# Delta rules: no dense products in the first seven steps of the meta tokens' chain, more of them in the four tiles' steps

## The reference, cut to what matters

```python
def gated_delta_rule(q, k, v, g, beta):          # chunks of 64, 8 heads
    ...
    kb = k * beta[..., None]
    lower = jnp.where(strict, jnp.einsum('nbhid,nbhjd->nbhij', kb, k) * decay, 0.0)
    rhs = jnp.concatenate([v * beta[..., None], kb * jnp.exp(g)[..., None]], axis=-1)
    sol = lax.linalg.triangular_solve(eye + lower, rhs, left_side=True, lower=True)
    u, w = sol[..., :DV], sol[..., DV:]
    ...
    def step(S, xs):
        v_new = u_c - jnp.einsum('bhcd,bhde->bhce', w_c, S)
        o = jnp.einsum('bhcd,bhde->bhce', qd_c, S) + jnp.einsum('bhij,bhje->bhie', attn_c, v_new)
        S = S * gl_c[..., None, None] + jnp.einsum('bhcd,bhce->bhde', kd_c, v_new)
        return S, o
```

## Time and profile before

| | us |
|---|---|
| median of 3 runs | 2184.63 |
| lowest and highest | 2182.49, 2186.39 |
| the profiled execution | 2186.5 |
| its span | 2184.7 |
| its mean granted TensorE clock | 0.984 |
| TensorE busy in the span | 2103.3 (96%) |
| first group's `delta_rule` | from 876.5 to 1061.6 |
| second group's `delta_rule` | from 1289.1 to about 1471 |

### The profile page before, as it was taken

One profiled execution on the slowest core, in us unless ns is written; L12 is line 12 of the kernel. 1 busy time (PEld: TensorE's weight loads), 2 busy tenths in 40 slices (PEclk: granted clock), 3 DMA queues, 4 the chain that ended last, 5 costly groups with the idle time before them and its releaser, 6 DMA issues. The chain is left out here.

```text
span 2184.7 us, 32900 instructions
## 1 busy us (share of the span) xinstructions
PE 2103.3 (96%) x13936; PEld 1681.0 (77%) x13936; DVE 1098.9 (50%) x1676; ACT 821.8 (38%) x1326; POOL 66.0 (3%) x69
## 2 busy tenths in 40 slices
PE   8979999999999899999999999999999899999999
PEld 6757678888888798666789976669786678888887
DVE  4544765777743366445355645444437544444422
ACT  4324554444432274222433532226436433222211
POOL 0011320000000000000000000000000000000000
PEclk9999999999999999999999999999999999999999
DMA  4331002333333321111223211113220232333222
GB/s 171 107 106 49 1 30 77 97 97 97 97 97 97 106 81 56 59 40 40 97 87 127 78 49 50 40 30 118 88 68 1 97 126 87 96 97 96 93 92 96
DMA packets 51426, 175.69 MB, mean 80 GB/s; under 512 B 6480, under 2 KB 10960, under 8 KB 50640
## 3 DMA queue, kind: packets, MB, share of 16 engines
q1 hardware_dynamic: 51280, 173.59, 24.6%
HBM read 164.07 MB, written 8.45 MB: 79 GB/s over the span
## 5 line engine op out<-in xcount | busy, mean ns | idle before, releaser
L280 PE MATMUL ps<-nx_hi,whi 128*128 128x512 f32 (+3 forms) x1696 | 574.8, 339 | 13.0 <-PEq L2204 6.3
L281 PE MATMUL ps<-nx_lo,whi 128*128 128x512 f32 (+3 forms) x1696 | 571.7, 337 | 0.0
L282 PE MATMUL ps<-nx_hi,wlo 128*128 128x512 f32 (+3 forms) x1696 | 570.7, 336 | 0.0
L266 ACT ACTIVATE whi<-raw 128x1024 fp32r<-128x1024 f32 x282 | 297.4, 1054 | 591.6 <-PE ps L282 545.8
L275 DVE TENSOR_TENSOR wlo<-raw,whi 128x1024 fp32r<-128x1024 f32 x282 | 344.4, 1221 | 261.0 <-ACT whi L266 260.7
L280 PEld LDWEIGHTS ps<-nx_hi,whi 128*128 128x128 f32 x1696 | 322.1, 190 | 57.2 <-DVE wlo L275 7.2
L281 PEld LDWEIGHTS ps<-nx_lo,whi 128*128 128x128 f32 x1696 | 321.9, 190 | 33.8
L282 PEld LDWEIGHTS ps<-nx_hi,wlo 128*128 128x128 f32 x1696 | 322.2, 190 | 33.4
L280 PE MATMUL ps<-mixer_out,whi 128*128 128x512 f32 x384 | 154.0, 401 | 5.8 <-PEq L2888 3.8
L282 PE MATMUL ps<-mixer_out,wlo 128*128 128x512 f32 x384 | 153.1, 399 | 0.0
L281 PE MATMUL ps<-mixer_out,whi 128*128 128x512 f32 x384 | 153.1, 399 | 0.0
(11 more groups left out here) (456 smaller groups left out, 2778.3 us busy)
## 6 DMA issues: line engine op xcount, KB each, us to landing
raw<-stream_dram SPq DMA_DIRECT2D x285, 512.0 KB, 3.5
arena<-keys_dram SPq DMA_DIRECT2D x1, 2112.0 KB, 9.3
h_sb<-x_dram SPq DMA_DIRECT2D x4, 512.0 KB, 6.7
mixer_floats<-cmp_w_k_dram SPq DMA_DIRECT2D x8, 256.0 KB, 4.0
mixer_floats<-cmp_w_v_dram SPq DMA_DIRECT2D x8, 256.0 KB, 4.5
h_dram<-h_sb SPq DMA_DIRECT2D x1, 2048.0 KB, 8.6
gate_dram<-arena SPq DMA_DIRECT2D x1, 2048.0 KB, 7.2
keys_dram<-h_sb SPq DMA_DIRECT2D x1, 2048.0 KB, 9.2
```

The lines of the kernel that those rows point to most:

```text
L266: act.activation(K.whi[:, n % HL], K.raw[:, n % RAW], ACT.Copy).then_inc(K.s_hi, 1)
L280: pe.matmul(out, whi, xhi, start=start, stop=False, skip_group_check=skip)
L281: pe.matmul(out, whi, xlo, start=False, stop=False, skip_group_check=skip)
L282: return pe.matmul(out, wlo, xhi, start=False, stop=stop, skip_group_check=skip)
```

## The change

The weights of the first seven points of the meta chain become zero; the eighth, "u_sb", keeps its 6. `SIDE_X` stays as it is. As the 360 dense matmuls of a group are shared out over a smaller sum of weights, the four tiles' points and "u_sb" get what the seven points no longer take.

```diff
-SIDE_META = {"ug": 4, "lower": 8, "a_sb": 4, "x2_sb": 4, "a4_sb": 4, "x8_sb": 4, "r_sb": 4, "u_sb": 6}
+
+SIDE_META = {"ug": 0, "lower": 0, "a_sb": 0, "x2_sb": 0, "a4_sb": 0, "x8_sb": 0, "r_sb": 0, "u_sb": 6}
 SIDE_X = {"ug": 4, "lower": 12, "a_sb": 4, "x2_sb": 4, "a4_sb": 4, "x8_sb": 4, "r_sb": 4, "k_sb": 4, "k2_sb": 4, "y_sb": 4,
           "w_sb": 4, "nw": 3, "vn 0": 4, "state 1": 4, "vn 1": 4}
```

## The result

The changed kernel takes 2199.34 us (median of 6 runs, 2196.12 to 2201.43) against 2184.53 of the kernel before (6 runs): the ratio is 1.0065, interval 1.0054 to 1.0077. It is slower, as forecast, but beyond the top of the range (2198.0). Two later comparisons gave 1.0051 (1.0037 to 1.0064) and 1.0058 (1.0046 to 1.0071). All runs of this study together have medians of 2198.5 (16 runs) and 2186.1 (93 runs), 12.4 us apart.

What follows compares the result with a forecast made beforehand. TensorE, busy 96%, was taken to bound the kernel through idle stretches and clock. Per group 1.6 us (8.0 tiles minus 6.4 meta chain) plus 3.3 for the clock, twice, made 9.7 on 2184.6: 2194, range 2187.5 to 2198.

Steps and rivals of the forecast that it cites:

- The tiles' term: In the four tiles: 37 moved dense matmuls cost 8.6 us, with changed idle stretches 8.0 us per group.
- tile 1's 1.87: Ahead of tile 1's L2314: a 1.87 us idle stretch, expected to go since no chunk ends at tile 0's end.
- rival (c): In each group one eviction in its new place isn't covered, 1.9 us on top: 2198; chance 0.05.
- The meta chain's latency: Meta chain without dense matmuls runs at its own latency: L2300 at 882.8 against 889.17, saving 6.4 us per group.
- the small batches: Meta chain's batches of 16-wide products, 2.6 us together: 0.5 us taken as their extra at the lower clock.
- 1.6 was the term: Net cost per group without the clock: 8.0 in the tiles minus 6.4 saved in the meta chain.
- The clock: In the nearly empty meta chain of both groups the granted clock falls to 0.50, costing 3.3 us per group.
- rival (a): Clock stays at 1.00 in the meta chain, only exposed latency is left: 2187.7, not measurably slower; chance 0.14.
- tile 3's new wait: Ahead of tile 3: VectorE's work from a chunk ending at tile 2's "state 1" leaves TensorE waiting 1.64 us.
- the falls in tiles: Two clock falls in the first group's tiles, 1.55 and 1.4 us, taken as likely after as before.
- Rival (b): Fuller tiles remove tile 3's wait and both clock falls in tiles, clock stays up in the meta chain: 2181.4; chance 0.04.
- the 5 that I had named as the upper end: Upper bound of the clock's price per group, in the meta chain, if L2306 is slow too.

Runs made afterwards that it cites:

- 19 and 37 idle-time matmuls: Changed kernel plus 19 or 37 dense-size matmuls, result unused, in each meta chain: 19 took 2193.58 and 2188.07 us, 37 took 2200.04 us.
- 12 idle-time matmuls: Changed kernel plus 12 dense-size matmuls, result unused, at the seven emptied points of each meta chain: 2198.57 us, ratio 1.0054 against the kernel before.
- the kernel before with other turns: Kernel before with u_sb's weight at 15 instead of 6, so no chunk ends at the last two points of tiles 0 to 2: 2181.86 us, ratio 0.9978.
- 15 real ones: Changed kernel with 15 useful dense matmuls put back in the meta chain's first seven points, 22 left in the tiles: 2187.79 us, ratio 1.0010.

## Why the prediction was right in kind and short in size

**The tiles' term.** 8.0 us worked out, 7.5 measured at full clock. That tile 1's 1.87 would go and tile 3 get 1.64 was read from the running sums; it is 1.66. No other eviction was uncovered, so rival (c) didn't happen.

**The meta chain's latency.** L2301 was put at 6.3 us behind the start at full clock and 6.5 to 7.5 at half; it is 6.6 to 6.7 in all traces. The chain built from distances of the old rows held step by step, each step within some 0.2 us. With the small batches 0.1 us slower at the lower clock and the old distance of 3.63 to L2307, L2307 would stand some 10.2 us behind the start at full clock (an estimate from these rows), so the meta chain saves 6.1 us, not 6.4. Without the clock's part a group then costs 7.5 - 6.1 = 1.4 us; 1.6 was the term.

**The clock, the step that failed.** It fell in both groups in each of three traces, so rival (a) is wrong. Its price up to L2307 is what was expected: from L2301 to L2307 6.7 to 6.8 us instead of 3.63, 0.1 in the small batches and up to 0.2 in L2307 itself make 3.2 to 3.4; 3.3 was the term, with too little of it put on L2301 and the matmuls behind it and too much on the small batches. What failed is that I put the fall behind tile 3's new wait at nothing. I had forecast that wait, and had rows in which a fall behind such a wait costs 1.4 to 1.55, but took the falls in tiles as no likelier after than before. In the kernel before the second group has none in three traces; in the changed kernel it has one behind tile 3's wait in all three, and so has the kernel with only the second group changed. Its price follows from the second stage: 191.3 - (185.1 + 7.5 - 2.8), the last being what L2307's place gained with the clock low (16.3 - 13.5), leaves 1.5. With the wait taken away the fall is gone too; but the wait alone doesn't bring it, since it stands in all four stages of the kernels with 19 and 37 idle-time matmuls without a fall. So the second group costs 6.2 us where 4.9 were forecast: 3.3 + 1.5 for the clock instead of 3.3, and 1.4 instead of 1.6 for the rest. Rival (b) had the fuller tiles wrong: tile 3's wait came in every trace.

In the first group the sum came out right by luck: its mean is 192.5 us against 187.7 before, 4.8 us, where 4.9 were forecast. The falls of the kernel before, which I had let stand and which cost 2.6 us there on the mean (187.7 - 185.1), are gone, and others stand in their place. In two of three traces the clock stayed down through L2307 to tile 0's head, and no fall follows at tile 3. The stage then takes 193.1, that is 3.3 more than 185.1 + 7.5 - 2.8, so with the 3.1 ahead of L2307 this one fall costs some 6.4 us, beyond the 5 that I had named as the upper end.

**The sum.** The stages' means differ by 11.0 us where 9.7 were forecast. These 1.3 are the second group's. The first comparison has 14.8 (2199.34 - 2184.53). Of the 3.8 beyond the stages, 2.4 are the draw of the executions, since all runs together are 12.4 apart. The last 1.4 us stay open. 0.6 of them stands between and behind the stages in the traces, without a known cause. The rest is less than what the start of the first stage moves by chance.

**The range.** Its top was 2198.0, one mishap above the likeliest sum. The likeliest case's own upper bound, 5 us of clock in each group, already reached 2197.7, and I added nothing for the luck of falls: within one series the executions of the kernel before lie 4 to 9 us apart, the slow ones at the lower mean clock (2190.3 us at 0.981, 2181.5 at 0.986).

**Rules of the skill.** The rule that activity releases the throttle (the Trainium skill, "TensorE: Matmul & The Clock Gate", "What's actually happening") spoke against this change, and the clock did fall in all six stages. But TensorE's busy time alone doesn't tell when: with 12 idle-time matmuls it fell behind 7.8 us in which TensorE was busy throughout, and in the kernel before with other turns behind 14.6. The floor of about 25 ns from start to start for small matmuls (the Trainium skill, same page, "Wait — 56ns, not 53.3ns?") fits the rows: at the full clock batches of 16 and 24 took 0.56 and 0.76 us, 25 ns for each one more; at the lower clock 0.58 and 0.80, 28 ns. So I had put too much on them (0.5 for all). These products are 16 columns wide, while the 256-column L2301 went from 1.90 to 3.59.

## What to carry to other kernels

Filler work isn't free to move even where it seems to pay only for latency: count what it hides (here 2.5 of 8.6 us per group: the 37 matmuls put L2307 at 16.3 us instead of some 10.2), and ask what the clock does once only narrow products are left. A dense product beside a chain of small ones has two effects. Here 15 matmuls hid the chain's waits, but with them the clock held in one group and fell in the other. Where work is shared out by a running sum, look where each piece ends: a piece that ended in the wrong place made TensorE wait 1.9 us per group, and moving the ends was the only edit here that made the kernel faster (2181.86 us against 2186.0).

## What the runs showed of the hardware that wasn't expected

The clock fell with TensorE busy for 7.8 of 7.8 us (12 wide matmuls among the small batches), and held with 19 in one trace of the same chain. It fell once behind 14.6 us without an idle stretch, with dense matmuls at every point (the kernel before with other turns, first group). In the second group of the kernel with 15 real ones it stayed low through 3.6 us of L2301, seven wide matmuls and 3.8 us of L2307. Why it fell or stayed low in these places, and not in the other group of the same kernel, stays open. And the same instructions in the same kernel took 182.5 us in one group and 189.6 in the other, with the clock as the only difference seen: one trace of a stage with sparse wide work tells little about its time.
